# A hybrid decoder layer on one Trainium2 core: the cached index keys are gathered behind the first feed-forward block and transposed in place

## The chip, the core and the metric

The kernel runs on one core of a Trainium2 chip. The metric is the device time of one execution in microseconds. Three timed runs of the kernel before gave 1490.46, 1493.34 and 1495.22 us; their median, 1493.34 us, is the number that the change is held against. The profile is of a further execution.

The engines are named as in the profile: PE is TensorE (PEld its weight loads), DVE is VectorE, ACT is ScalarE, POOL is GpSimd and SP is SyncE. SP computes nothing here, it issues DMAs. ACT and POOL issue DMAs too. All of them run on the core's 16 DMA engines.

## The reference

One layer is computed for 512 prompt tokens and for 64 sample tokens (8 sequences with 8 new tokens each, behind a paged cache of 4096 past tokens per sequence).

```
x = x + 0.5 * SwiGLU(RMSNorm(x))                     # first feed-forward block
h = RMSNorm(x); q, k, v, qi, ki, wi, ... = h @ w_in
ki_all = concat([cache_idx_k[page_table], ki])       # sample: 4096 past index keys of 32 numbers
dots   = einsum('thd,sd->ths', qi, ki_all)           # 8 index heads
scores = einsum('th,ths->ts', wi, relu(dots))
idx    = top_k(scores)                               # 256 keys per sample token
att    = softmax(q . k[idx]) v[idx]                  # gathered from cache_k, cache_v
x = x + (gate_c * conv(h) + gate_a * att @ w_aout) @ w_o
x = x + 0.5 * SwiGLU(RMSNorm(x))                     # second feed-forward block
```

The change is about `cache_idx_k[page_table]`. It is 256 pages (8 sequences with 32 pages) of 128 keys with 32 float32 numbers, 16 KB a page, 4.19 MB together. Both feed-forward blocks are 1024 to 2816 and back, in float32.

## The kernel before, in words

The program is written out by hand for each engine: the order of the code is the order on the engine, and semaphores tie the engines together. The first 168 us, the only part that the change touches, go like this.

**The sample's feed-forward block and projections.** SP streams weights in units of 512 KB through ten slots (six of the tile `ring`, two of `w_raw`, two of `spare`), in the order in which they are used. The helper `stream` (L414) issues a unit when the semaphore `ring_used` says that the unit before in its slot was used. 82 units pass: 44 of the first matrix, 22 of the second, and 16 of `w_in`, in groups of four that here are called g0 (index columns, 296 wide, so 303 KB a unit), g1 (queries), g2 (keys) and g3 (values). On PE `stream_mm` (L635) multiplies the 64 sample rows by a unit (four matmuls in the profile's count of a 512-wide unit) and raises `ring_used`. So `ring_used` stands at 66 when the feed-forward block is through, at 70 after g0, 74 after g1 and 82 after g3. Behind unit 66 come the residual sum and the norm (DVE L2146, ACT L1453, PE L844 and L773, DVE L2087) before g0 can start.

**Work between the units.** After the first eight units PE transposes the prompt's rows (`xnp` to `xT`, L817), after units 32 it sums the prompt's squares (`prompt_sums`, L623), and after each eight units it transposes the sample's activations (`turn_a`, L782).

**The index keys.** POOL gathers one page a partition with an indirect DMA. The first gather (L2793, half of the sequences, 2.1 MB into the tile `ikn`) is issued as soon as the page table is in; the second (L2802, into the same tile) when the first half has been transposed. `turn_ik` (L795) transposes `ikn` on PE in blocks of 128x128, four to a PSUM bank, in banks 6 and 7 by turns, 16 blocks a call; there are four calls, between the units of the feed-forward block. `evac_ik` (ACT L1473) copies each bank to `ikT`.

**The small trip of the weights.** The index weights `wi` come out of g0. DVE computes the index projections (L2092 to L2191) and raises `iro_ready`. POOL then writes the weights to DRAM (`wi_scratch`, L2805) and reads them back in another layout (`wv`, L2808). DVE makes the matrices `wst` from them (L2212), then the terms of the new keys (`newrel`, L2218), and raises `S_ready`.

**The index products.** `new_dots` (L866, L869) multiplies for the new keys; its results lie in banks 4 to 7 until `newrel` is done. Then `dots(n)` for n = 0 to 15 (L886) multiplies the queries by the cached keys, banks 0 to 3 by turns, ACT takes the ReLU (L1532), and `scores_w(u)` (L897) sums the heads with `wst`. `dots` 0 to 7 need the first half of the keys, 8 to 15 the second. Behind `scores_w(3)` the prompt's first feed-forward block starts (L647).

## Time and profile before

| | us |
|---|---|
| median of three runs | 1493.34 |
| the profiled execution | 1504.95 |
| its span (first to last instruction) | 1503.2 |
| PE busy in the span | 1425.7 (95%) |
| DVE busy | 1052.6 (70%) |
| POOL busy | 592.7 (39%) |
| ACT busy | 546.1 (36%) |
| last matmul of the sample's feed-forward block ends | 118.2 |
| first matmul of the prompt's feed-forward block starts | 167.55 |

All times below are us from the start of the span. Busy shares are averages over stages with different limits: in the first 118 us the DMA engines are full and PE waits in places, from 167.55 on PE is busy nearly without a gap. A time in the table of a stage therefore says more than the 95%.

### The profile page before, as it was taken

How to read it: one execution, taken by the hardware profiler on the slowest of the kernel's cores; microseconds unless marked ns; L12 is line 12 of the kernel's file. 1: busy time of each engine (PE TensorE's matmuls, PEld its weight loads, DVE VectorE, ACT ScalarE, POOL GpSimd, SP SyncE). 2: the span in 40 equal slices, each digit the busy share in tenths (PEclk: the TensorE clock that was granted, in tenths of full speed). 3: DMA queues.
4: the chain of work that ended last, by engine and by line, in shares of the span. 5: the costliest groups of instructions: out<-in, count | busy, mean ns of one | idle time of the engine just before them, and what ended most of it. 6: DMA issues, size and time to landing. Idle time of an engine off the chain costs nothing. (4 is left out here: it accounts for less than half of the span.)

```text
span 1503.2 us, 20865 instructions
## 1 busy us (share of the span) xinstructions
PE 1425.7 (95%) x8219; PEld 1121.6 (75%) x8219; DVE 1052.6 (70%) x1684; ACT 546.1 (36%) x838; POOL 592.7 (39%) x415
## 2 busy tenths in 40 slices
PE   4998999999999999999899899899998999999998
PEld 2333578877888875436666565689998999999998
DVE  1256788989836898999996997657779755774221
ACT  1332655335712331122112234543364444453111
POOL 2000465454379855543345776122304454320000
PEclk8998999999999999999999999999999999999999
DMA  9997254232257988878458766432422323312222
GB/s 342 370 380 245 87 95 106 92 95 74 71 183 245 286 254 284 284 213 271 126 168 278 256 212 217 144 119 85 126 71 71 107 78 97 113 43 78 79 91 84
DMA packets 156930, 248.75 MB, mean 165 GB/s; under 512 B 11965, under 2 KB 104909, under 8 KB 156571
## 3 DMA queue, kind: packets, MB, share of 16 engines
q1 hardware_dynamic: 131742, 164.22, 34.1%
q0 software_dynamic: 23104, 76.16, 16.1%
q10 hardware_dynamic: 1989, 7.07, 1.2%
q8 instruction: 63, 1.03, 0.3%
q14 instruction: 32, 0.26, 0.1%
HBM read 237.58 MB, written 10.20 MB: 165 GB/s over the span
## 5 line engine op out<-in xcount | busy, mean ns | idle before, releaser
L2782 POOL TENSOR_TENSOR w_lo<-w_raw,w_hi 128x1024 fp32r<-128x1024 f32 x65 | 171.5, 2638 | 221.4 <-ACT w_hi L1330 221.1
L696 PE MATMUL ps<-bh,wqr 128*128 128x288 f32 x936 | 205.3, 295 | 4.2 <-DVE wqr L1940 2.0
L2849 POOL DMA_INDIRECT kv<-cache_v,idxT x128 | 138.6, 1083 | 96.6 <-PE ps L1108 45.7
L1330 ACT ACTIVATE w_hi<-w_raw 128x1024 fp32r<-128x1024 f32 (+1 forms) x88 | 91.3, 1037 | 227.3 <-PE ps L647 148.1
L2837 POOL DMA_INDIRECT kv<-cache_k,idxT x128 | 138.6, 1083 | 86.7 <-DVE kprod L2475 54.6
L696 PEld LDWEIGHTS ps<-bh,wqr 128*128 128x128 f32 x936 | 155.5, 188 | 5.0 <-DVE wqr L1940 3.9
L647 PE MATMUL ps<-h_hi,w_hi 128*128 128x512 f32 x352 | 139.3, 396 | 2.1 <-POOL w_lo L2782 2.1
L647 PE MATMUL ps<-h_hi,w_lo 128*128 128x512 f32 x352 | 137.4, 390 | 0.0
L647 PE MATMUL ps<-h_lo,w_hi 128*128 128x512 f32 x352 | 137.2, 390 | 0.0
L712 PE MATMUL ps<-a_hi,wqr 128*128 128x288 f32 x704 | 122.3, 295 | 0.0
L696 PE MATMUL ps<-bl,wqr 128*128 128x288 f32 x384 | 113.2, 295 | 0.0
L1093 PE MATMUL ps<-h,wn 128*128 128x288 f32 x448 | 111.1, 407 | 0.3 <-ACT sgb L1682 0.3
L1058 PE MATMUL ps<-wn,xg 128*128 128x512 f32 (+1 forms) x256 | 103.1, 563 | 4.0 <-ACT rp L1663 2.1
L1093 PEld LDWEIGHTS ps<-h,wn 128*128 128x128 f32 x448 | 84.2, 190 | 26.6 <-issue 1.9
L712 PEld LDWEIGHTS ps<-a_hi,wqr 128*128 128x128 f32 x704 | 103.1, 188 | 0.0
L1953 DVE TENSOR_TENSOR wqr<-wq,wqr 128x1024 fp32r<-128x1024 f32 (+1 forms) x24 | 27.2, 1135 | 95.1 <-ACT wqr L1368 95.1
L2914 POOL TENSOR_TENSOR wq<-wq 128x1024 f32<-128x1024 f32 x10 | 24.9, 2490 | 172.5 <-PE ps L696 76.7
L2475 DVE TENSOR_TENSOR kprod<-kv,qb 128x1024 f32<-128x1024 f32 x64 | 84.4, 1319 | 9.9 <-issue 3.3
L1058 PEld LDWEIGHTS ps<-wn,xg 128*128 128x128 f32 x256 | 49.6, 196 | 55.2 <-issue 49.0
L1215 PE MATMUL ps<-h,wn 128*128 128x288 f32 x320 | 83.9, 413 | 2.4 <-issue 2.4
L647 PEld LDWEIGHTS ps<-h_hi,w_hi 128*128 128x128 f32 x352 | 66.4, 189 | 18.1 <-issue 3.3
L2478 DVE TENSOR_REDUCE G<-kprod 128x16 f32<-128x1024 f32 x64 | 78.2, 1222 | 2.2
(513 smaller groups left out, 3190.6 us busy)
## 6 DMA issues: line engine op xcount, KB each, us to landing
w_raw<-w_ffn_in SPq DMA_DIRECT2D x56, 512.0 KB, 11.8
wq<-w_ffn_in SPq DMA_DIRECT2D x40, 512.0 KB, 3.6
wn<-w_in SPq DMA_DIRECT2D x36, 512.0 KB
qb<-q_scratch SPq DMA_DIRECT2D x64, 256.0 KB
ring<-w_ffn_in SPq DMA_DIRECT2D x28, 512.0 KB
w_raw<-w_ffn_out SPq DMA_DIRECT2D x24, 512.0 KB, 9.8
wq<-w_ffn_out SPq DMA_DIRECT2D x20, 512.0 KB
ring<-w_ffn_out SPq DMA_DIRECT2D x14, 512.0 KB
```

The source lines that it names most:

```text
L647: mm = pe.matmul(ps[:, 2 * half + m, :], w[:, k, m * P:(m + 1) * P], x[:, kc0 + k, c0:c0 + SEQ], start=(first and k == 0 and fst), stop=(l ...
L696: mm = pe.matmul(ps[:, bank + m, 0:HALF], w[:, k, m * P:(m + 1) * P], b[:, j, k, :], start=(j in (0, 1, 5) and k == 0 and fst), stop=(k == ...
L712: mm = pe.matmul(ps[:, 4 * half + 2 * m + hf_, 0:HALF], w[:, k, m * P:(m + 1) * P], x[:, kc0 + k, hf_ * HALF:(hf_ + 1) * HALF], start=(kc0 ...
L1058: mm = pe.matmul(ps[:, s % 8, 0:n], xg[:, kk, P * b:P * b + P], wt[:, k, :], start=(kk == 0), stop=(kk == KD - 1))
L1093: mm = pe.matmul(ps[:, 4 * half + 2 * m + hf_, 0:HALF], wt[:, k, m * P:(m + 1) * P], h32[:, 4 * (n % 2) + k, hf_ * HALF:(hf_ + 1) * HALF], ...
L1215: mm = pe.matmul(ps[:, hf_, 0:HALF], wt[:, k % 4, m * P:(m + 1) * P], h32[:, k, hf_ * HALF:(hf_ + 1) * HALF], start=(k == 0), stop=(k == K ...
L1330: act.activation(w_hi[:, slot, 0:n], w_raw[:, slot, 0:n], ACT.Copy).then_inc(S_("hi_ready"), 1)
L2475: dve.tensor_tensor(kprod[:, :, :], kv[:, n % KV, :, :], qb[:, j, :].unsqueeze(1).to_broadcast([P, 2, DA]), ALU.mult)\
L2478: dve.tensor_reduce(G[:, :, n], kprod[:, :, :].rearrange("p c (h d) -> p (c h) d", h=H), AX.X, ALU.add).then_inc(S_("logits_ready"), 1)
L2782: pool.tensor_tensor(w_lo[:, slot, 0:n], w_raw[:, slot, 0:n], w_hi[:, slot, 0:n].bitcast(F32), ALU.subtract)\
L2837: pool.indirect_dma_start(kv[:, n % KV, c, :], None, rows[0], bass.IndirectOffsetOnAxis(ap=idxT[:, c, n:n + 1], axis=0))\
L2849: pool.indirect_dma_start(kv[:, V_SLOT[j % 3] + a // 2, a % 2, :], None, rows[1], bass.IndirectOffsetOnAxis(ap=idxT[:, j % 2, t:t + 1], ax ...
```

## The change

The tile `ikn` goes. The gathers write straight to `ikT`, each half to its own part, and the transposes read a block of `ikT` and are copied back over the same block. The first gather is issued when `ring_used` is at 66, the second at 74 and when the first has landed. The transposes of the first half stand on PE between g0 and g1 (two calls of 16), those of the second half between the index products: 16 behind `dots(3)`, 16 behind `dots(5)`. The wait for `S_ready`, which stood behind `dots(7)`, moves with them behind `dots(3)`, since the transposes write banks 6 and 7. The transposes of the norm move to banks 4 and 5.

```diff
-        (ikn,), _ = place(m1, [("ikn", (P, PAGE * ID), F32)])
...
-                        mm = pe.transpose(ps[:, 6 + n_tr[0] % 2, j * P:(j + 1) * P], ikn[:, kg * P:(kg + 1) * P], ident[:, :])
+                        mm = pe.transpose(ps[:, 6 + n_tr[0] % 2, j * P:(j + 1) * P], ikT[:, gseq, kg, :], ident[:, :])
...
-                if t in (1, 2):
-                    turn_ik(0, 4 * t - 4)
-                if t in (4, 5):
-                    turn_ik(1, 4 * t - 16)
...
-            pe.wait_ge(S_("ikT_evac"), 16)
...
+                if g == 0:
+                    turn_ik(0, 0)
+                    turn_ik(0, 4)
...
+            pe.wait_ge(S_("ikT_evac"), 8)
             for n in range(16):
                 dots(n)
+                if n == 3:
+                    pe.wait_ge(S_("S_ready"), 1)
+                    turn_ik(1, 0)
+                if n == 5:
+                    turn_ik(1, 4)
                 if n == 7:
-                    pe.wait_ge(S_("S_ready"), 1)
+                    pe.wait_ge(S_("ikT_evac"), 16)
                     pe.wait_ge(S_("qbd_ready"), 2)
...
             act.activation(h32[:, :, 0:NS], hTs[:, :, :], ACT.Copy).then_inc(S_("hhi_ready"), 1)
+            evac_ik(0, 0)
+            evac_ik(0, 4)
...
+                if n == 3:
+                    evac_ik(1, 0)
+                if n == 5:
+                    evac_ik(1, 4)
...
-            pool.indirect_dma_start(ikn[:, :], None, ik_rows, bass.IndirectOffsetOnAxis(ap=ptile[:, 0:1], axis=0)).then_inc(S_("ik_in"), 16)
...
-            pool.wait_ge(S_("ikT_evac"), 8)
-            pool.indirect_dma_start(ikn[:, :], None, ik_rows, bass.IndirectOffsetOnAxis(ap=ptile[:, 1:2], axis=0)).then_inc(S_("ik_in"), 16)
+            for g, used_up in enumerate((66, 74)):
+                pool.wait_ge(S_("ring_used"), used_up)
+                if g:
+                    pool.wait_ge(S_("ik_in"), 16)
+                pool.indirect_dma_start(ikT[:, g, :, :].rearrange("p a b -> p (a b)"), None, ik_rows, bass.IndirectOffsetOnAxis(ap=ptile[:, g:g + 1], axis=0))\
+                    .then_inc(S_("ik_in"), 16)
 
             pool.wait_ge(S_("iro_ready"), 1)
             pool.dma_start(wi_dram, wisc[0:NS, 0, :]).then_inc(S_("wv_in"), 16)
```

In the order of the program the changed places look like this. Each row is one instruction or a run of equal ones, in the order of its engine; `[waits ...]` lists the semaphores it waits for. On PE, from the third unit of g0 (units 64x296, `hTs` is the sample's normed rows) to the start of g1, there stands before:

```order
L635 MATMUL ps<-spare,hTs 64x296 [waits ring8]
L635 MATMUL ps<-spare,hTs 64x296
L635 MATMUL ps<-spare,hTs 64x296 [waits ring9]
L635 MATMUL ps<-spare,hTs 64x296
L635 MATMUL ps<-ring,hTs 64x512 [waits ring0]
L635 MATMUL ps<-ring,hTs 64x512
L635 MATMUL ps<-ring,hTs 64x512 [waits ring1]
```

In the changed kernel the same place reads:

```order
L634 MATMUL ps<-spare,hTs 64x296 [waits ring9]
L634 MATMUL ps<-spare,hTs 64x296
L794 MATMUL ps<-ident,ikT 128x128 [waits ik_in]
L794 MATMUL ps<-ident,ikT 128x128 x7
L794 MATMUL ps<-ident,ikT 128x128 [waits ikT_evac]
L794 MATMUL ps<-ident,ikT 128x128 x3
L794 MATMUL ps<-ident,ikT 128x128 [waits ikT_evac]
L794 MATMUL ps<-ident,ikT 128x128 x3
...
L794 MATMUL ps<-ident,ikT 128x128 [waits ikT_evac]
L794 MATMUL ps<-ident,ikT 128x128 x3
L634 MATMUL ps<-ring,hTs 64x512 [waits ring0]
```

32 transposes of the first half now stand between g0 and g1, and the first one waits for the first gather (`ik_in`).

On PE among the index products (`qbd` holds the queries, `iTp` the queries for the new keys), from the end of `new_dots` to `dots(4)`, there stands before:

```order
L869 MATMUL ps<-iT,iTp 128x64 x8
L886 MATMUL ps<-ikT,qbd 128x512 x2
L886 MATMUL ps<-ikT,qbd 128x512 [waits choice_step]
...
L886 MATMUL ps<-ikT,qbd 128x512 [waits scored]
L886 MATMUL ps<-ikT,qbd 128x512
L886 MATMUL ps<-ikT,qbd 128x512 [waits scored]
L886 MATMUL ps<-ikT,qbd 128x512
L886 MATMUL ps<-ikT,qbd 128x512 [waits scored]
```

and now:

```order
L865 MATMUL ps<-iT,iTp 128x64 x8
L882 MATMUL ps<-ikT,qbd 128x512 [waits ikT_evac]
L882 MATMUL ps<-ikT,qbd 128x512
L882 MATMUL ps<-ikT,qbd 128x512 [waits choice_step]
...
L882 MATMUL ps<-ikT,qbd 128x512 [waits scored]
L882 MATMUL ps<-ikT,qbd 128x512
L794 MATMUL ps<-ident,ikT 128x128 [waits ikT_evac,ik_in,S_ready]
L794 MATMUL ps<-ident,ikT 128x128 x3
L794 MATMUL ps<-ident,ikT 128x128 [waits ikT_evac]
L794 MATMUL ps<-ident,ikT 128x128 x3
...
L882 MATMUL ps<-ikT,qbd 128x512 [waits scored]
L882 MATMUL ps<-ikT,qbd 128x512
```

The first transpose of the second half stands between `dots(3)` and `dots(4)` and waits for `S_ready` and for the second gather. Before, the products ran on here, and `S_ready` was awaited four products later.

On POOL, from the last small constant to the read of `wv`, there stood before:

```order
L2800 DMA gkb<-g_k 128x64
L2802 DMA ikn<-cache_idx_k,ptile 128x4096 [waits ikT_evac]
L2805 DMA wi_scratch<-wisc 64x8 [waits iro_ready]
L2808 DMA wv<-wi_scratch 64x8x1 [waits wv_in]
L2808 DMA wv<-wi_scratch 64x8x1
```

and now:

```order
L2803 DMA gkb<-g_k 128x64
L2808 DMA ikT<-cache_idx_k,ptile 128x4096 [waits ring_used]
L2808 DMA ikT<-cache_idx_k,ptile 128x4096 [waits ik_in,ring_used]
L2812 DMA wi_scratch<-wisc 64x8 [waits iro_ready]
L2815 DMA wv<-wi_scratch 64x8x1 [waits wv_in]
L2815 DMA wv<-wi_scratch 64x8x1
```

Between `gkb` and `wi_scratch` there are now two gathers, the second of which waits for g1; `wi_scratch` is behind it on the same queue.

## Rows read from the trace of the kernel before

**Rows 1.** The page, the span in 40 equal slices (tenths busy).

```profile
PE   4998999999999999999899899899998999999998
DMA  9997254232257988878458766432422323312222
```

**Rows 2.** Windows: length, busy us by engine (PE to POOL), PEclk, DMA, GB/s.

```profile
52.00:56.00 4.00, 4.00 (x18) 1.22 (x16) 0.76 (x2) 0.00 (x0) 0.00 (x0) 0.87 0.66 193
56.00:118.00 62.00, 57.19 (x278) 21.90 (x274) 27.01 (x39) 17.16 (x31) 1.01 (x1) 1.00 1.05 385
118.00:126.00 8.00, 2.47 (x20) 1.91 (x20) 4.92 (x9) 1.92 (x5) 0.00 (x0) 0.70 0.99 365
137.00:144.00 7.00, 7.00 (x50) 2.77 (x46) 4.51 (x8) 0.00 (x0) 1.41 (x2) 1.00 0.17 32
```

**Rows 3.** PE in time, the first 118 us (start, duration, line, tiles, wait).

```profile
48.34 1.14 PE L795 MATMUL ps<-ident,ikn 128*128 128x128 f32 x8 [2.26 <-ACT ikT L1473]
...
82.74 1.09 PE L795 MATMUL ps<-ident,ikn 128*128 128x128 f32 x8
84.09 1.14 PE L795 MATMUL ps<-ident,ikn 128*128 128x128 f32 x8 [0.25 <-ACT ikT L1473]
...
117.11 1.08 PE L635 MATMUL ps<-ring,aTs 128*64 128x512 f32 x4 [0.18 <-DMA ring<-w_ffn_out]
```

**Rows 4.** PE in time, from the norm to the prompt's first matmul.

```profile
125.93 2.24 PE L635 MATMUL ps<-w_raw,hTs 128*64 128x296 f32 x8 [0.78 <-DVE hTs L2087]
129.93 4.39 PE L635 MATMUL ps<-ring,hTs 128*64 128x512 f32 x16
134.25 0.40 PE L854 MATMUL ps<-ident,iros 64*128 64x64 f32 x3
135.08 1.94 PE L635 MATMUL ps<-ring,hTs 128*64 128x512 f32 x8
142.09 0.39 PE L866 MATMUL ps<-wisc,permm 64*128 64x8 f32 x2
143.01 1.99 PE L886 MATMUL ps<-ikT,qbd 64*128 64x512 f32 x8
...
147.52 2.04 PE L886 MATMUL ps<-ikT,qbd 64*128 64x512 f32 x8 [0.21 <-ACT relu_b L1532]
...
167.55 0.50 PE L647 MATMUL ps<-h_hi,w_hi 128*128 128x512 f32 x1
```

**Rows 5.** Windows of 46 to 130, columns as in rows 2.

```profile
46.00:48.00 2.00, 0.08 (x1) 0.00 (x0) 1.90 (x4) 0.82 (x2) 0.00 (x0) 1.00 1.06 390
50.00:52.00 2.00, 2.00 (x6) 0.69 (x8) 0.00 (x0) 0.41 (x2) 0.00 (x0) 0.50 1.00 371
122.00:130.00 8.00, 5.66 (x31) 3.23 (x31) 3.50 (x5) 1.81 (x5) 0.00 (x0) 0.50 0.71 244
```

**Rows 6.** DMA issues of the first 125 us (KB each, median us to landing).

```profile
ikn<-cache_idx_k,ptile POOLq DMA_INDIRECT x2, 11.8
permm<-c_perm POOLq DMA_DIRECT2D x1, 32.0 KB, 11.6
gkb<-g_k POOLq DMA_DIRECT2D x1, 32.0 KB, 13.3
...
wv<-wi_scratch POOLq DMA_DIRECT2D x2, 2.0 KB, 2.5
wi_scratch<-wisc POOLq DMA_DIRECT2D x1, 2.0 KB, 5.5
```

**Rows 7.** DVE in time, from the value rows to the new keys' sums.

```profile
143.91 1.66 DVE L2212 TENSOR_SCALAR wst<-spread,wv 128x128 f32<-128x128 f32 x8 [0.22 <-DVE vns L2093]
...
146.81 1.03 DVE L2223 TENSOR_REDUCE newsum<-newrel 128x64 f32<-128x512 f32 x1
```

**Rows 8.** POOL in time, the trip of the weights.

```profile
133.85 0.56 POOL L2805 DMA_DIRECT2D wi_scratch<-wisc  x1 [71.00 <-DVE iros L2187]
139.61 1.41 POOL L2808 DMA_DIRECT2D wv<-wi_scratch  x2 [5.20 <-DMA wi_scratch<-wisc]
```

More of the change, by code:

```diff
@@ L830, in _ @@
                     pe.wait_ge(S_("ones_ready"), 1)
-                    pe.wait_ge(S_("ikT_evac"), 8)
                     prompt_sums(0, 6, sqp)
@@ L841, in _ @@
             pe.wait_ge(S_("x1_ready"), 1)
-            pe.wait_ge(S_("ikT_evac"), 16)
             for k in range(KD):
-                mm = pe.transpose(ps[:, 6, k * NS:(k + 1) * NS], xs[:, k * P:(k + 1) * P], ident[0:NS, 0:NS])
+                mm = pe.transpose(ps[:, 5, k * NS:(k + 1) * NS], xs[:, k * P:(k + 1) * P], ident[0:NS, 0:NS])
             mm.then_inc(S_("hsT_done"), 1)
-            turn_h(1, 7)
+            turn_h(1, 4)
             pe.wait_ge(S_("hTs_ready"), 2)
@@ L1496, in _ @@
             silu_s(1)
-            evac_ik(0, 0)
             evac_a(0)
             silu_s(2)
-            evac_ik(0, 4)
             evac_a(1)
@@ L1504, in _ @@
             silu_s(4)
-            evac_ik(1, 0)
             evac_a(3)
             silu_s(5)
-            evac_ik(1, 4)
             evac_a(4)
@@ L1515, in _ @@
             act.wait_ge(S_("hsT_done"), 2)
-            act.activation(xT[:, :, 0:NS], ps[:, 6, :].rearrange("p (k n) -> p k n", k=KD), ACT.Copy).then_inc(S_("iTp_ready"), 1)
+            act.activation(xT[:, :, 0:NS], ps[:, 5, :].rearrange("p (k n) -> p k n", k=KD), ACT.Copy).then_inc(S_("iTp_ready"), 1)
             act.wait_ge(S_("hTs_ready"), 2)
             act.activation(h32[:, :, 0:NS], hTs[:, :, :], ACT.Copy).then_inc(S_("hhi_ready"), 1)
+            evac_ik(0, 0)
+            evac_ik(0, 4)
             act.wait_ge(S_("iT_done"), 1)
@@ L2151, in _ @@
             dve.wait_ge(S_("gm_in"), 16)
-            sample_norm(1, gmc, 7)
+            sample_norm(1, gmc, 4)
             link(dve.memset(qbd[:, :, :, :], 0.0))
```

## The prediction

> **What bounds the kernel now.** I read the page's slices first, then windows, then each engine in time. In the slices PE is at nine tenths or more nearly everywhere from the fifth slice on, while the DMA engines are full only in the first three [rows 1]. The windows say what that means. From 56 to 118 us the DMA engines are full (share 1.05) at 385 GB/s, and PE has 57.19 of 62 us [rows 2]; the last units are each waited for on a DMA [rows 3]. So up to 118.19 us (117.11 + 1.08) the bytes set the time. I call this moment E; the last matmul of the sample's feed-forward block ends there. From E to 125.93 the norm runs (DVE, ACT and PE in turns), and from there PE works through g0 to g3 and the index products to 167.55 with small gaps [rows 4]. This stretch, 49.36 us long, is a chain of PE, ACT and the small trip of the index weights. The DMA engines have holes in it: 32 GB/s from 137 to 144 us [rows 2]. Behind 167.55 PE hardly waits, and everything there (the search for the keys on DVE, the gathers of keys and values) hangs on the scores or on PE's own progress. I take it that what the start of the prompt's block moves, the end moves by the same amount.
>
> So there are two sums: how much earlier E comes, and how much longer than 49.36 us the stretch behind it becomes.
>
> **The first 118 us.** The two gathers leave. They are 2 x 128 x 16 KB = 4.19 MB, which at 385 GB/s [rows 2] is 10.9 us. With them leave 64 transposes on PE and 16 copies on ACT. These cost nothing where PE waits for DMA anyway, but once they cost something: at 46 to 48 us PE sat 2.26 us behind ACT [rows 3], its clock then stood at half level (1.2 GHz, 0.50 in 50 to 52 us) [rows 5], slots came free late, and the DMA engines moved 193 GB/s from 52 to 56 us [rows 2], a loss of 4 x (385 - 193) = 0.77 MB, 2.0 us. That stop goes too. Nothing else is late in its place: the sums of the squares stop PE for 7 us, but up to ten units are under way, ten times 0.52 MB / 385 GB/s = 13.6 us. Gain: 12.9 us, which I call at least 10.9 less a microsecond, should a new stop appear, and at most 14.
>
> **From E to the end of g1.** The norm and g0 stay: g0 ends at E + 11.7 (129.93). The first gather is issued at E. A gather beside a busy SP queue took 11.8 us to land [rows 6], and SP's queue is busy here too (365 GB/s from 118 to 126 [rows 2]), so it lands at E + 11.9. PE waits 0.2 us; bounds 0 and, with 13.3 us as for the last DMA behind a gather [rows 6], 1.6 us. The weights of g1 share the engines with it: what was still to come at E is 8 x 365 GB/s = 2.9 MB [rows 2], with the gather's 2.1 MB 5.0 MB, 13 us at 385 GB/s, so they are in before g1 needs them. The six units of g2 and g3 that are still to load, 3.1 MB, take until E + 21, and PE comes to them from E + 22 on. Then 32 transposes. 16 of them took 2.49 us (82.74 to 85.23) with ACT copying behind [rows 3], so 32 take 5.0. But after the pause of the norm the clock is at half level (0.50 from 122 to 130 us) [rows 5], and g0 pays 4.0 us for what takes half of it at full level. What g1 paid for warming up, 4.32 us (129.93 to 134.25) for what takes 3.5 (half of the 7.0 from 135.08 to 142.09) [rows 4], the transposes pay now: 0.9 more. On DVE the index projections (before under g1) now run under these transposes, and on ACT the copies are done 3 us before the next thing it is wanted for. The transposes end at E + 17.8 and g1, now 3.5 us, at E + 21.3.
>
> **To dots(3).** As before: 0.83 us of transposes (134.25 to 135.08), 7.01 for g2 and g3, 0.92 for new_dots, 4.51 for four products (143.01 to 147.52) [rows 4]: PE is behind dots(3) at E + 34.6.
>
> **The wait that the change adds.** Behind dots(3) PE now waits for S_ready, which needs newrel, which needs wst, which needs wv, which needs the trip of the weights through DRAM. Before, POOL issued the trip at 133.85, E + 15.7, and read back at 139.61 [rows 8]; wst started at 143.91, set by the value rows on DVE and not by wv (the trip was in by 139.61 + 0.7 + 2.5 = 142.8). Now POOL stands first at its wait for g1 (E + 21.3), then issues the second gather (1 us), then wi_scratch, on the same queue. DMAs issued on POOL's queue behind the first gather landed 11.6 us (the third behind it) to 13.3 us after their issue [rows 6], where small ones with nothing large ahead took 2.5 to 5.5: they came in behind the gather. So the trip waits for the second gather.
>
> How long a gather takes with the DMA engines nearly free no row shows. Below it is 2.1 MB / 385 GB/s = 5.4 us and 1.5 us of start and end (less than the 2.5 us of wv), 6.9; above it is 11.8, the one beside a full SP queue. I take 8.7, with the bytes alone and 3.3 us around them. It lands at E + 30.0, wi_scratch 1.0 later, wv 3.2 behind that (0.7 + 2.5) at E + 34.2, and wst to newrel take 2.9 (143.91 to 146.81) [rows 7]: S_ready at E + 37.2. PE stands from 34.6 to 37.2, 2.6 us. Queued behind the waiting transpose is the rest of the products, and with them scores, keys and the prompt's block.
>
> The page DMA: Bandwidth & Descriptors of the Trainium skill (section Anatomy of one DMA) gives a DMA of POOL's path 2.0 us and its bytes at 436 GB/s, which as an estimate is 6.8 us for this gather; the trace has only the 11.8 us with company, so it neither bears the rule out nor contradicts it. By it the wait would be 0.7 us, and the sum 1.9 us smaller and without the clock's share below, 1491.4 in all; that is rival 1.
>
> **From the wait to 167.55.** The 16 transposes take 2.4 us, dots(4) and dots(5) follow, then 16 more, paced by ACT, which has the ReLU and the copies in one queue: 2.6. Together 5.0 on top of the 20.03 us that the rest took (147.52 to 167.55) [rows 4]. A stop of 2.26 us was followed by half clock from about 50 to 53 us [rows 3, 5]; a stop of 2.6 us does the same here, over the transposes and two products: 1.3 us for the transposes, 1 for the products, 2.3 in all. Bounds 0 (no drop) and 4.
>
> **The sum.** The stretch is now 37.2 + 5.0 + 20.0 + 2.3 = 64.5 us against 49.36, so 15.2 longer; E is 12.9 earlier. Net +2.3 us. In the profiled execution, that is 1504.95 + 2.3 = 1507.3. It stands 11.6 us above the median of the runs; I carry the difference over: 1493.3 + 2.3 = 1495.6. A difference under 0.3%, 4.5 us, a measurement of this kernel can't tell from none.
>
> **The rivals.**
> 1. *The added wait ends early* (the gather takes 6.9 us alone, the lower bound, or wi_scratch gets past it). For it: the DMA engines are nearly idle then. Then S_ready comes at E + 35.4 at the latest, PE stops for 0.8 us or not at all, its clock stays, and without any stop 34.6 + 25.0 = 59.6, +10.2, less 12.9: -2.7 us, 1490.6. With a gain of 14 in the first part 1489.5.
> 2. *Slower: the second gather sets the path fully.* If it takes 11.8 us as beside SP's queue, S_ready comes at E + 40.3, PE stands for 5.7 us, and the clock's share is 4: 69.3, +20.0, less 12.9: +7.1, 1500.4. It decides from a landing of about 10 us on. For it: the only two gathers seen took that; against it: SP's queue has only two units of 0.5 MB left then.
> 3. *The opening gives less* (10 us, because some other stop in the stream takes over from the bytes, so that the change doesn't do there what it says). For it: the engines were not full at 52 to 56 us. Then +5.2, 1498.5.
>
> **How the numbers follow.** Forecast 0.42, rival 1 0.27, rival 2 0.17, rival 3 0.14. The forecast's own range is 1493 to 1498. The range for 8 in 10 reaches from 1489 (rival 1 with the larger gain) to 1501 (rival 2). Faster by more than 4.5 us needs rival 1 and more: 0.14. Slower by more than that: rival 2, half of rival 3, and a little of the forecast: 0.27. Within: 0.59.
>
> **What would show it.** In the changed profile: E at 105.3 and no stop near 46 us; DMA share near 1.05 up to E; the first transpose of keys within 1 us behind g0; the second gather's landing 8.7 us after its issue; wi_scratch landing behind it; wst starting on DVE behind wv and not behind the value rows; a wait of 2 to 3 us on PE ahead of the first transpose behind dots(3), put down to DVE newrel; half clock right behind it; the prompt's first matmul at 169.9. The forecast is wrong if E stays above 108, if the wait at dots(3) is missing or over 5 us, or if the part behind 168 us changes its length by more than 1 us.

## The result and the profile after

The changed kernel took 1496.98 us (median of 19 runs, 1491.98 to 1500.53) beside 1494.07 us for the kernel before on the same chip (19 runs, 1488.97 to 1498.05). The ratio is 1.0022, 95% interval 1.0013 to 1.0031: 1.9 to 4.6 us slower, which is little but more than nothing by this interval. The profiled execution of the changed kernel took 1496.92 us, its span is 1493.8.

The two rows of the page's slices look almost as in [rows 1]. No slice differs by more than a tenth but the third of PE, which fell from 9 to 7:

```profile
PE   5978999999999999999999999999998999999998
DMA  9996254322256889868448877432321322312222
```

The windows that answer to [rows 2], the third moved with the end of the sample's block:

```profile
52.00:56.00 4.00, 3.18 (x14) 0.59 (x12) 1.37 (x2) 0.63 (x1) 0.00 (x0) 1.00 1.05 388
56.00:104.00 48.00, 43.02 (x188) 13.61 (x186) 22.02 (x31) 9.32 (x16) 0.00 (x0) 1.00 1.05 377
106.00:114.00 8.00, 2.41 (x20) 1.83 (x22) 4.70 (x9) 2.45 (x5) 0.93 (x1) 0.76 1.08 420
137.00:144.00 7.00, 3.13 (x16) 1.46 (x16) 3.81 (x14) 3.52 (x6) 0.00 (x0) 1.00 0.25 78
144.00:146.00 2.00, 1.95 (x10) 1.63 (x12) 1.93 (x4) 1.16 (x3) 0.00 (x0) 0.56 0.00 0
```

The hole at 52 to 56 us is gone. From 137 to 144 us PE, which had all of the 7 us before, has 3.13. From 144 to 146 us the granted clock is 0.56. PE in time says why; these rows answer to [rows 3] and [rows 4]:

```profile
104.54 1.08 PE L634 MATMUL ps<-ring,aTs 128*64 128x512 f32 x4 [0.18 <-DMA ring<-w_ffn_out]
...
113.41 2.24 PE L634 MATMUL ps<-w_raw,hTs 128*64 128x296 f32 x8 [0.78 <-DVE hTs L2091]
...
117.35 1.09 PE L794 MATMUL ps<-ident,ikT 128*128 128x128 f32 x8
118.69 1.15 PE L794 MATMUL ps<-ident,ikT 128*128 128x128 f32 x8 [0.25 <-ACT ikT L1475]
...
122.51 3.65 PE L634 MATMUL ps<-ring,hTs 128*64 128x512 f32 x16
126.10 0.40 PE L850 MATMUL ps<-ident,iros 64*128 64x64 f32 x3
...
137.11 2.04 PE L882 MATMUL ps<-ikT,qbd 64*128 64x512 f32 x8 [0.27 <-ACT relu_a L1532]
142.70 1.09 PE L794 MATMUL ps<-ident,ikT 128*128 128x128 f32 x8 [3.55 <-DVEq L2226]
...
145.81 2.88 PE L882 MATMUL ps<-ikT,qbd 64*128 64x512 f32 x8
...
169.16 0.50 PE L646 MATMUL ps<-h_hi,w_hi 128*128 128x512 f32 x1
```

E is 104.54 + 1.08 = 105.62. The first transpose follows g0 without a wait, and the one real stop is the 3.55 us behind `dots(3)`. DVE and POOL over the same stretch answer to [rows 7] and [rows 8]:

```profile
139.84 1.65 DVE L2216 TENSOR_SCALAR wst<-spread,wv 128x128 f32<-128x128 f32 x8 [4.30 <-DMA wv<-wi_scratch]
...
142.74 1.06 DVE L2227 TENSOR_REDUCE newsum<-newrel 128x64 f32<-128x512 f32 x1
```

```profile
105.91 1.02 POOL L2808 DMA_INDIRECT ikT<-cache_idx_k,ptile  x1 [91.21 <-PE ps L634]
126.45 0.98 POOL L2808 DMA_INDIRECT ikT<-cache_idx_k,ptile  x1 [19.52 <-PE ps L634]
127.44 0.58 POOL L2812 DMA_DIRECT2D wi_scratch<-wisc  x1
135.26 1.43 POOL L2815 DMA_DIRECT2D wv<-wi_scratch  x2 [7.24 <-DMA wi_scratch<-wisc]
```

Read from the bottom up: `wv` waits 7.24 us for `wi_scratch`, which was issued right behind the second gather; `wst` waits 4.30 us for `wv`; PE waits 3.55 us for DVE. The issues' landing times, which answer to [rows 6]:

```profile
permm<-c_perm POOLq DMA_DIRECT2D x1, 32.0 KB, 5.3
gkb<-g_k POOLq DMA_DIRECT2D x1, 32.0 KB, 6.8
ikT<-cache_idx_k,ptile POOLq DMA_INDIRECT x2, 9.9
wv<-wi_scratch POOLq DMA_DIRECT2D x2, 2.0 KB, 4.1
wi_scratch<-wisc POOLq DMA_DIRECT2D x1, 2.0 KB, 7.5
```

The 9.9 is the mean of 11.4 (first gather, beside SP's stream) and 8.4 (second). `wi_scratch` took 7.5 where it took 5.5 before, and the small constants, which now have no gather ahead of them, 5.3 and 6.8 where they took 11.6 and 13.3.

### The profile page after: what moved, and what is told of

Same layout as the page of the kernel before. It is cut to its first block and busy times, and to the rows that moved or that the text cites. A ratio compares the mean times of both kernels' runs of the same rounds, so it can differ in the third digit from the quotient of the medians.

```text
span 1493.8 us, 20865 instructions
## 1 busy us (share of the span) xinstructions
PE 1424.8 (95%) x8219; PEld 1119.5 (75%) x8219; DVE 1051.3 (70%) x1684; ACT 546.0 (37%) x838; POOL 592.1 (40%) x415
```

## The experiments

"Start" is the first matmul of the prompt's feed-forward block, "stretch" is E to start. But for the two first profiles, each kernel was timed 12 times (both gathers early: 6) beside the kernel before on the same chip, in three groups of four on one chip each. Times are us from the start of the span. The runs with the second gather out, with the second half out and with the second half not transposed leave work out and compute wrong scores for half of the sequences; they serve the times only.

| kernel | ratio to before, 95% | E | stretch | start |
|---|---|---|---|---|
| before, first profile | | 118.19 | 49.36 | 167.55 |
| before, again | 0.9999 [0.9982, 1.0016] | 115.93 | 49.47 | 165.40 |
| changed, first profile | 1.0022 [1.0013, 1.0031] | 105.62 | 63.54 | 169.16 |
| changed, again | 1.0031 [1.0016, 1.0045] | 105.74 | 63.97 | 169.71 |
| trip ahead of the second gather | 0.9995 [0.9982, 1.0007] | 104.94 | 59.55 | 164.49 |
| trip on SP's queue | 1.0001 [0.9988, 1.0014] | 106.72 | 59.85 | 166.57 |
| second half not transposed | 1.0000 [0.9986, 1.0014] | 104.90 | 57.04 | 161.94 |
| both gathers early | 1.0058 [1.0038, 1.0077] | 115.05 | 59.32 | 174.37 |
| before, first calls later | 0.9990 [0.9977, 1.0002] | 115.07 | 48.88 | 163.95 |
| ... and last call in the norm's gap | 0.9995 [0.9982, 1.0008] | 115.31 | 49.19 | 164.50 |
| ... and idle products in the gap | 0.9982 [0.9971, 0.9994] | 115.19 | 48.46 | 163.65 |
| before, second gather out | 0.9981 [0.9968, 0.9995] | 114.26 | 49.21 | 163.47 |
| before, second half out | 0.9991 [0.9977, 1.0004] | 114.26 | 49.26 | 163.52 |
| one half each | 1.0020 [1.0007, 1.0033] | 113.73 | 55.52 | 169.25 |

**Both kernels again.** The changed kernel, unedited:

> The changed kernel once more, beside the kernel before on the same chip, as the base for the three others. My theory: 12.6 us less in the opening and 14.2 us more between the end of the sample's feed-forward block and the prompt's block, so about 2 to 3 us slower than before (ratio 1.0015 to 1.002). Rival (the two profiles differ by 1.6 us at the start of the prompt's block and the timed runs by 2.9, so something behind that point is slower too): ratio 1.0022 or more and a later part that is longer.

And the kernel before, unedited:

> The kernel before, unchanged, with a profile of its own beside the others. The first profile of it is 1503.2 us long, and the part behind the start of the prompt's block is 1335.6 us there, but 1324 to 1327 us in the profiles of the changed kernel and its variants, while the timed runs say that before is the faster. My theory: that first profiled execution was a slow one behind 168 us, and the part is as long in both kernels; here it is 1324 to 1327 us, the prompt's block starts at 166.5 to 167.6, and the timed ratio is 1.000. Rival: the part behind 168 us is really longer in the kernel before, again 1333 us or more, and the changed kernel gets something back there.

The changed kernel repeated its profile: E 105.74, stop 3.56 us, half clock behind it. The kernel before did not: E came 2.3 us earlier than in its first profile, and behind the start it took 1325.4 us (1490.8 - 165.40) where the first profile has 1335.6 (1503.2 - 167.55). The hole at 52 to 56 us was smaller, after the same stop of 2.26 us:

```profile
52.00:56.00 4.00, 4.00 (x20) 1.26 (x18) 1.37 (x2) 0.33 (x1) 0.00 (x0) 1.00 0.92 308
```

Over the 12 us in which the hole lies, 48 to 60, the repeat moved 356 GB/s and the first profile 317. Against 385 that is 0.35 MB and 0.82 MB, or 0.9 and 2.1 us:

```profile
48.00:60.00 12.00, 11.75 (x60) 5.64 (x59) 3.88 (x6) 3.79 (x7) 0.00 (x0) 0.88 0.99 356
```

So the first profile, on which the sum was made, shows a larger hole than the repeat does, by 1.2 us of the 2.3 us between the two E. Against the repeat the changed kernel starts the prompt's block 3.8 and 4.3 us later, and the timed medians differ by 2.9 and 3.2. Five profiles have the changed kernel's opening (its own two, the two of the trip, and the second half not transposed), and their E lies between 104.90 and 106.72. A difference of a microsecond in E can't be read from one pair of profiles alone. Most of this spread is again a hole, just behind the sums of the squares. In the order second half not transposed (E 104.90), changed (105.62) and trip on SP's queue (106.72):

```profile
64.00:76.00 12.00, 12.00 (x68) 4.95 (x69) 4.97 (x8) 1.01 (x2) 0.00 (x0) 1.00 1.07 366
64.00:76.00 12.00, 12.00 (x64) 4.88 (x64) 4.37 (x7) 1.01 (x2) 0.00 (x0) 1.00 1.04 347
64.00:76.00 12.00, 12.00 (x62) 4.76 (x63) 4.16 (x7) 1.01 (x2) 0.00 (x0) 1.00 1.03 322
```

Against 385 GB/s these lack 0.6, 1.2 and 2.0 us. The kernel before has no such hole there: its repeat moved 401 GB/s in the same 12 us, with the second gather under way.

**The trip of the weights ahead of the second gather.** On POOL only the order is changed:

```diff
+            pool.wait_ge(S_("ring_used"), 66)
+            gather_ik(0)
             pool.wait_ge(S_("iro_ready"), 1)
             pool.dma_start(wi_dram, wisc[0:NS, 0, :]).then_inc(S_("wv_in"), 16)
...
+            pool.wait_ge(S_("ring_used"), 74)
+            pool.wait_ge(S_("ik_in"), 16)
+            gather_ik(1)
```

> The changed kernel, with the trip of the index weights through DRAM issued on POOL's queue before the second gather. My theory: the trip is late because POOL stands first at its wait for g1 and then because the small DMAs land behind the gather; with the order turned, wst is set by the value rows again, PE doesn't stop at dots(3) (3.55 us in the changed kernel), its clock stays at full level there (about 1.2 us), and the second gather, issued 1.4 us later, still lands before dots(3) ends. So 4.7 us less than the changed kernel, ratio to before about 0.999. Rival: the wait at dots(3) is for the gather of the second half itself (it takes 8.4 us), then the stop stays at 2 us or more.

```profile
120.64 0.56 POOL L2813 DMA_DIRECT2D wi_scratch<-wisc  x1 [14.39 <-DVE iros L2191]
125.67 1.42 POOL L2816 DMA_DIRECT2D wv<-wi_scratch  x2 [4.46 <-DMA wi_scratch<-wisc]
127.38 1.02 POOL L2806 DMA_INDIRECT ikT<-cache_idx_k,ptile  x1 [0.30 <-issue]
```

On DVE, and on PE the first transposes behind `dots(3)`:

```profile
135.94 1.66 DVE L2216 TENSOR_SCALAR wst<-spread,wv 128x128 f32<-128x128 f32 x8 [0.22 <-DVE vns L2097]
```

```profile
139.27 1.09 PE L794 MATMUL ps<-ident,ikT 128*128 128x128 f32 x8
```

`wst` again stands behind the value rows, as in [rows 7], PE does not stop, the clock stays, and the gather, issued 0.9 us later, is still in before its transposes. The stretch is 4.0 and 4.4 us shorter than in the two profiles of the changed kernel, and the timed ratio is back at 1. This shows that the place on POOL's queue costs the changed kernel about all that it loses. Two things change together, and this run doesn't part them: the write is issued 6.8 us sooner (120.64 instead of 127.44), since POOL no longer waits for g1 first, and it lands 4.7 us after its issue instead of 7.5.

**The trip on SP's queue.** SP, which streams the weights, issues it behind the last of them instead of POOL:

```diff
+            sp.wait_ge(S_("iro_ready"), 1)
+            sp.dma_start(wi_dram, wisc[0:NS, 0, :]).then_inc(S_("wv_in"), 16)
+            sp.wait_ge(S_("wv_in"), 16)
...
-            pool.wait_ge(S_("iro_ready"), 1)
-            pool.dma_start(wi_dram, wisc[0:NS, 0, :]).then_inc(S_("wv_in"), 16)
```

> The changed kernel, with the trip of the index weights issued by SP, which is through with its weights by then, and both gathers issued on POOL exactly as in the changed kernel. My theory: the trip lands 3 to 5 us after its issue although the gathers fill the engines, since it is no longer behind them in one queue; no stop at dots(3); 4.7 us less than the changed kernel. Rival (the trip is late since the engines are full, not since it is queued): the trip's write takes 7 us here too, S_ready comes about 2 us earlier only because POOL's wait is gone, and the stop stays at 1 us or more.

SP came to it only when slots were free for its last loads. The write went out 1.55 us ahead of the second gather (127.45), and the read back ran beside it:

```profile
125.90 0.48 SPq L483 DMA_DIRECT2D wi_scratch<-wisc  x1
130.20 1.65 SPq L486 DMA_DIRECT2D wv<-wi_scratch  x2
```

The two reads of `wv` landed 5.6 and 7.9 us after their issue, `wst` began at 138.83 behind a wait of 2.30 us for them, PE stopped for 1.55 us, and the clock did not fall. This is not the same trip on another queue, however: SP's version breaks it into 1040 packets more. Up to 150 us the profile counts 27111 packets here, 2944 of them under 512 B, against 26071 and 1904 in the changed kernel, for the same bytes. From 134.5 to 138 us, with all but 0.08 MB of the gather through, over a thousand packets under 512 B still passed. So the late read doesn't show what a gather's company costs a small transfer, nor does this run show that `wi_scratch` would land sooner beside a gather on another queue.

**The second half not transposed.** In the changed kernel both calls of the second half and their copies are out; the waits for `S_ready` and for the second gather stay. Products 8 to 15 multiply untransposed keys.

```diff
                 if n == 3:
                     pe.wait_ge(S_("S_ready"), 1)
-                    turn_ik(1, 0)
-                if n == 5:
-                    turn_ik(1, 4)
+                    pe.wait_ge(S_("ik_in"), 32)
```

> The changed kernel without the transposes of the second half and their copies on ACT; the waits for S_ready and for the second gather stay behind dots(3) (the products 8 to 15 multiply keys that are not transposed). My theory: the transposes between the products are worth 5.0 us on the path and the stop is a cost of its own, so the stop at dots(3) stays at 3.5 us, the clock falls all the same, and the prompt's block starts 4 to 5 us earlier than in the changed kernel, at about 164.7; ratio to before about 0.9995. Rival: the transposes are half hidden behind ACT's ReLU, then it starts only 2.5 us earlier.

```profile
136.42 2.04 PE L882 MATMUL ps<-ikT,qbd 64*128 64x512 f32 x8 [0.27 <-ACT relu_a L1529]
141.90 1.99 PE L882 MATMUL ps<-ikT,qbd 64*128 64x512 f32 x8 [3.44 <-DVEq L2219]
```

From 141.90 to the start it took 20.04 us, against 26.46 (142.70 to 169.16) in the changed kernel: 6.4 us, where 4 to 5 were expected. Without a stop, in the kernel with the trip ahead of the gather, 25.22 us pass from the end of `dots(3)` to the start, so the transposes are 5.2 us of it, and the clock the other 1.2. (In the repeat of the changed kernel the clock's share is 0.7 by the same sum: 169.71 - 143.82 = 25.89.) The clock stayed up here, after a stop of 3.44 us:

```profile
138.00:144.00 6.00, 2.45 (x12) 0.69 (x8) 4.57 (x15) 2.46 (x3) 0.00 (x0) 1.00 0.00 0
```

The timed ratio of 1.0000 is not as low as the start, 3.5 us earlier than before's, would make it; that is the one place where start and time part by more than 1.2 us, and it stays open.

**The first calls of transposes one round later,** in the kernel before (and the copies with them):

```diff
-                if t in (1, 2):
-                    turn_ik(0, 4 * t - 4)
+                if t in (2, 3):
+                    turn_ik(0, 4 * t - 8)
```

> The kernel before, with the first two calls of the transposes moved one round of eight units later, and their copies on ACT with them. My theory: the stop of PE at 46 us and the hole of the DMA engines at 52 to 56 us (0.77 MB, 2.0 us) are the second term of the gain in the opening, apart from the bytes. Without the stop the end of the sample's feed-forward block comes 2.0 us earlier and the whole is 2 us faster than before (ratio 0.9987). Rival (only the bytes of the gathers count): no change.

```profile
48.00:60.00 12.00, 11.75 (x64) 4.94 (x62) 4.90 (x8) 3.08 (x6) 0.00 (x0) 1.00 1.05 387
```

The stop and the slow clock behind it are gone, the hole too, and E is 0.9 us earlier than in the repeat of before. That is as much as the repeat's own hole is worth, so 0.9 us is taken as what the stop of [rows 3] costs there; the sum had 2.0, from the larger hole of the first profile.

**The second gather left out,** in the kernel before. The second half is transposed from the rows of the first, so half of the sequences are scored with other keys.

```diff
-            pool.indirect_dma_start(ikn[:, :], None, ik_rows, bass.IndirectOffsetOnAxis(ap=ptile[:, 1:2], axis=0)).then_inc(S_("ik_in"), 16)
```

> The kernel before without its second gather; the second half of the keys is transposed from the first half's rows, so all work of PE and ACT stays and only 2.1 MB of DMA leave (the scores of half of the sequences are of other keys). My theory: the bytes set the end of the sample's block, 2.1 MB at 385 GB/s are 5.4 us, so the block ends at 112.8, the prompt's block starts at 162.1, and the ratio to before is 0.9964. Rival: PE with its transposes and stops has a share in the bound, then 3 us or less.

2.1 MB less, 5.4 us at 385 GB/s, moved E by only 1.7 us. A hole opened elsewhere:

```profile
72.00:84.00 12.00, 11.75 (x54) 4.75 (x53) 4.03 (x6) 1.83 (x4) 0.00 (x0) 1.00 0.89 280
```

PE is busy throughout; my reading is that it gives slots back late, so that SP can't issue. In these 12 us the DMA engines could have moved 4.62 MB (385 GB/s) and moved 280 x 12 = 3.36 MB. The missing 1.26 MB are 3.3 us, where the repeat of before (368 GB/s) lacks 0.5. The hole at 52 to 60 was larger as well (314 GB/s against 349), by 0.7 us. Together 3.5 us, nearly the 3.7 that E lacks.

**The second half out of the opening altogether,** in the kernel before: neither gathered nor transposed; products 8 to 15 use the first half's keys.

```diff
-                if t in (4, 5):
-                    turn_ik(1, 4 * t - 16)
...
-            pool.indirect_dma_start(ikn[:, :], None, ik_rows, bass.IndirectOffsetOnAxis(ap=ptile[:, 1:2], axis=0)).then_inc(S_("ik_in"), 16)
```

> The kernel before without the second gather and without the 32 transposes of the second half (products 8 to 15 multiply the first half's keys again, so half of the sequences are scored with other keys). With only the gather taken out E came 1.7 us earlier where its bytes are 5.4 us, and the DMA engines had a hole at 72 to 84 us. Theory (the hole was PE's doing: the transposes and the sums of the prompt's squares kept PE from giving slots back): with the transposes gone as well the bytes bind again, E comes 5.4 us earlier than in the repeated run of the kernel before, at about 110.5, no hole over 1 us worth at 72 to 84, prompt's first matmul at 159.9, ratio 0.9963. Rival (the sums of the squares alone bind there): E at 112.5 to 113.5, the hole stays, ratio 0.998.

My theory fell: E is 114.26 as in the run above, and most of the hole is there.

```profile
72.00:84.00 12.00, 12.00 (x58) 4.65 (x58) 3.69 (x6) 1.01 (x2) 0.00 (x0) 1.00 0.94 308
```

That the two E agree to the hundredth is chance. The hole is 2.4 us here and 3.3 above, where the first 16 of the second half's transposes (81.85 to 84.27) fall into its end; in return the hole at 52 to 60 us, in which the two kernels do the same work, was larger here (293 GB/s against 314), by 0.4 us. By these holes the second half's 32 transposes cost half a microsecond to one, and what makes most of the hole is ahead of them: the sums of the squares, and perhaps the first half's transposes.

**Both gathers early, transposes as changed.** From the changed kernel:

```diff
             ik_rows = inp["cache_idx_k"].rearrange("o n p d -> (o n) (p d)")
+            gather_ik(0)
...
+            pool.wait_ge(S_("ring_used"), 32)
+            pool.wait_ge(S_("ik_in"), 16)
+            gather_ik(1)
```

> The changed kernel with one thing undone: both gathers are issued in the opening (the first when the page table is in, the second when 32 units of the stream are used), while the 64 transposes stay where the change puts them. The trip of the index weights then has no gather ahead of it on POOL's queue. Theory (the trade is bytes in the opening against transposes in the stretch, and the second gather's place costs a stop of 3.6 us and a slow clock of 1.2 us on top): E, the end of the sample's feed-forward block, goes back by both gathers' bytes, to 115.5 to 116.5 us; no stop behind dots(3); E to the prompt's first matmul takes what the kernel with the trip ahead of the second gather took, 59.5 us; the prompt's first matmul at 175 to 176; ratio to the kernel before 1.006 to 1.007. Rival (without the transposes in the opening PE gives slots back soon enough that part of the gathers' bytes passes unseen): E at 112 to 113, prompt's first matmul at 172, ratio 1.004.

E goes back by 9.4 us (105.62 to 115.05; 9.3 from the repeat), between theory and rival and nearer to the theory. Behind `dots(3)` PE went on at once:

```profile
147.18 2.04 PE L882 MATMUL ps<-ikT,qbd 64*128 64x512 f32 x8 [0.27 <-ACT relu_a L1532]
149.16 1.09 PE L794 MATMUL ps<-ident,ikT 128*128 128x128 f32 x8
```

The bytes of two gathers are 10.9 us. Of the other 1.5, 1.1 pass in time that the stream could not use: the changed kernel's DMA engines moved 370 GB/s from 64 to 90 us, those of this kernel 386, which is 0.42 MB more:

```profile
64.00:90.00 26.00, 23.36 (x102) 8.28 (x104) 9.76 (x15) 4.09 (x7) 0.84 (x1) 1.00 1.05 386
```

**One half each.** The first half is gathered and transposed in the opening (its calls one round later), the second half is gathered when `ring_used` is at 66, ahead of the trip, and transposed between the products.

```diff
+            gather_ik(0)
...
+                if t in (2, 3):
+                    turn_ik(0, 4 * t - 8)
...
+            pool.wait_ge(S_("ring_used"), 66)
+            gather_ik(1)
             pool.wait_ge(S_("iro_ready"), 1)
             pool.dma_start(wi_dram, wisc[0:NS, 0, :]).then_inc(S_("wv_in"), 16)
```

> One half as before, one half as changed: the first half is gathered and transposed in the opening (its two calls one round later than before), the second half is gathered at the end of the sample's feed-forward block, ahead of the trip of the index weights on POOL's queue but with the whole of g0 to g3 before its transposes, which stand between the products. Theory (each half costs about 5.4 us of bytes in the opening or about 5.2 us of transposes in the stretch, so that where it stands is nearly the same): E at 110.4, stretch 54.7, prompt's first matmul at 165.1, no stop behind dots(3) over 1 us, ratio 0.9993 to 1.0. Rival (the trip queued behind the gather is late here too, wi_scratch landing 7 us or more after its issue, and stops PE behind dots(3) by 2 us or more): prompt's first matmul at 167 to 168, ratio 1.001. Other rival (with half the transposes gone from the opening PE also spares the stops there): E at 109, ratio 0.998.

Both rivals and the theory missed: no stop behind `dots(3)`, but E only at 113.73, 3.3 us later than the bytes say, and the kernel is slower than before. (In the stretch PE also waits 1.0 us for the last weights of g3.) The stream from 64 to 90 us, in the changed kernel (first) and in this one:

```profile
64.00:90.00 26.00, 24.62 (x124) 8.57 (x122) 15.90 (x22) 6.88 (x11) 0.00 (x0) 1.00 1.05 370
```

```profile
64.00:90.00 26.00, 25.08 (x128) 10.91 (x125) 10.24 (x15) 6.17 (x11) 0.00 (x0) 1.00 0.95 324
```

And what PE does there:

```profile
63.68 1.09 PE L794 MATMUL ps<-ident,ikT 128*128 128x128 f32 x8
...
66.90 7.10 PE L622 MATMUL ps<-sqp,ones 128*128 128x512 f32 x16 [0.34 <-issue]
```

Transposes and sums keep PE from the stream for 10.3 us in a row (63.68 to 73.94). The sums alone, in the changed kernel, left 370 GB/s. With the same transposes and sums and the second gather issued at 66.73, right at the sums (the kernel before with the first calls later), it was 386. The gather needs no slot, so its bytes can pass just then. In the repeat of before it is issued 7 us ahead of the sums and still under way in them:

```profile
60.87 1.01 POOL L2802 DMA_INDIRECT ikn<-cache_idx_k,ptile  x1 [44.98 <-ACT ikT L1473]
```

So the gather fills the hole that transposes and sums make. With neither in the opening E is at 105.6; with one gather and 32 transposes at 113.7, 8.1 us more; with both halves (first calls later) at 115.1, only 1.3 more, where the second gather's bytes are 5.4. The reading that each half costs the same wherever it stands is wrong: 8.1 and 1.3 us are further apart than the 1.8 by which E varies.

**The last call in the norm's gap.** From the kernel with the first calls later:

```diff
-                if t in (4, 5):
-                    turn_ik(1, 4 * t - 16)
+                if t == 5:
+                    turn_ik(1, 0)
...
+            turn_ik(1, 4)
             pe.wait_ge(S_("x1_ready"), 1)
```

> The kernel of e3 (the kernel before with the first two calls one round later), with the last call of 16 transposes moved behind the last unit of the sample's feed-forward block, where PE waits for the residual sum and the norm. My theory: PE's clock falls to half level since PE has next to nothing to do from 118 to 126 us, and g0 pays 2 us and g1 0.8 us for it; the transposes are free there and shorten the pause, so the clock stays up or is back sooner, and the prompt's block starts 1.5 to 2.8 us earlier than in e3, ratio 0.9975. Rival: what is left of the pause (3 us and more with 16 small transposes in it) still brings the clock down, no gain over e3.

E did not move (115.31 beside 115.07), and 2.5 us of work at the head of the gap did not hold the clock (0.57 over 120 to 128 us, 0.62 without it). The rival held.

**Idle products in the gap,** on the same base: 18 ahead of the first transposes of the norm, 10 behind them and 4 behind the second ones (the profile counts two for each).

```diff
+            idle_products(18)
             pe.wait_ge(S_("x1_ready"), 1)
...
+            idle_products(10)
             turn_h(1, 7)
+            idle_products(4)
```

> The kernel before with the two first calls of transposes one round later, and 32 idle 128x128 products of PE (results unused, written to a bank that is free) in the pauses of the norm behind the sample's feed-forward block; their number fills most of the pauses of about 6 us. Theory (the half clock under g0 and g1, 0.50 from 122 to 130 us before, comes from PE's pause in the norm): the granted clock stays at 2.4 GHz, g0 and g1 together take 2.0 to 2.8 us less, E unchanged at 115, stretch 46.9, prompt's first matmul at 161.5, ratio 0.9973. Rival 1 (the clock falls in spite of idle products, since they leave pauses between them): same as without them, ratio 0.999. Rival 2 (g0 is held by ACT and DVE or by its weights, not by the clock): clock up, but g0 and g1 start no earlier and end within 1 us of before, ratio 0.9985.

```profile
122.00:130.00 8.00, 7.96 (x56) 4.21 (x54) 5.75 (x14) 0.63 (x1) 0.00 (x0) 1.00 0.70 244
```

```profile
119.34 0.71 PE L850 MATMUL ps<-ident,xs 64*128 64x64 f32 x8
119.98 2.50 PE L844 MATMUL ps<-ones,ident 128*128 128x128 f32 x20
122.41 0.71 PE L773 MATMUL ps<-ident,hns 64*128 64x64 f32 x8
...
124.13 1.22 PE L635 MATMUL ps<-w_raw,hTs 128*64 128x296 f32 x8
```

The granted clock is 1.00 throughout, where the same kernel without the products had 0.50 from 120 to 126 us, and g0 takes 2.05 us (124.13 to 126.18) where it took 3.65 there (122.82 to 126.47). That is 1.6 us (g1 takes 3.60 in both), less than the 2.0 to 2.8 expected of the two, and the products stood in the way: the norm's first transposes began 4.2 us behind E instead of 3.2, and g0 8.9 instead of 7.7 us behind it. So 1.2 us of the 1.6 went there, and the stretch is only 0.4 us shorter than without them. This kernel has the lowest ratio of those that compute everything, 0.9982 to before; its interval overlaps that of the same kernel without the products (0.9990), so the timed runs don't show the 0.4 us. Fewer products might keep more of it; that wasn't tried.

## Why the prediction was right, and where a size was off

The forecast was 1495.6 us, slightly slower than before and within 0.3% of it; the kernel took 1496.98 beside 1494.07. The chain from E to the prompt's block was the forecast one. The gain of the opening was not.

- *E 12.9 us earlier.* 12.57 against the first profile, but 10.2 and 10.3 against the repeat. This is the mis-sized term, by 2.6 us against the repeat. Bytes: 10.9 predicted, 9.4 measured (both gathers early). The stop near 46 us: 2.0 predicted, 0.9 measured (first calls later). 9.4 + 0.9 = 10.3; each is a difference of two profiles, while E of one and the same opening varied by 1.8. Two steps failed. One priced the whole low rate at 52 to 56 us from one profile [rows 2]. The other put the sums of the squares at nothing ("nothing else is late in its place", since ten units under way would last 13.6 us): the five profiles of the changed opening lack 0.5 to 2.0 us of bytes just behind the sums, a hole that the second gather filled before. So the bytes were not the bound everywhere.
- *First gather in at E + 11.9, PE waits 0.2.* It landed at 117.3, E + 11.7, and no matmul of PE waited for it.
- *Transposes 5.0 + 0.9, g1 out at E + 21.3.* 5.16 us for the 32 in the first profile (117.35 to 122.51) and 5.93 in the repeat (117.68 to 123.61), where the clock came back later. g1 ended at E + 20.5 and + 21.5, `dots(3)` at E + 33.5 and + 34.5 (predicted 34.6).
- *Second gather 8.7 us.* 8.4. The rule of the Trainium skill (DMA: Bandwidth & Descriptors, section Anatomy of one DMA), 6.8 by the estimate made from it, was 1.6 us too low: the measurement decides.
- *`wi_scratch` 1.0 behind it, `wv` 3.2, then 2.9.* 7.5 us from issue, so it came in almost with the gather; from `wv`'s issue to `wst` 4.6 us (135.26 to 139.84) instead of 3.2; 2.9 from `wst` to `newsum`. These errors nearly cancel: S_ready at E + 37.1, predicted 37.2 (E + 38.1 in the repeat, with g1 a microsecond later).
- *Stop 2.6 us, clock 2.3.* 3.55 and 1.2 (3.56 and 0.7 in the repeat). Both ends of the stop hang on the end of g1, so an earlier or later g1 doesn't change it. From there S_ready took 16.6 us in both profiles where the sum had 15.9, and PE was behind `dots(3)` after 13.05 where it had 13.3. The clock stayed down over fewer instructions. Together 4.75 and 4.2 against 4.9. With the trip ahead of the gather the stop is 0 and the stretch 59.6 (the 59.6 that the prediction gives for the case without a stop).
- *Stretch 64.5.* 63.5 and 64.0.
- *Net +2.3.* +1.6 against the first profile and +3.8 to +4.3 against the repeat; +2.9 and +3.2 by the timed runs. That the number came out so close is partly luck: the opening gave 2.6 us less than the sum had, and the stretch, 14.1 and 14.5 us longer instead of 15.2, took back 0.7 to 1.1 of it.
- *What the start moves, the end moves.* Good as a rule, not exact: behind the start the 13 profiles other than the first took 1323.0 to 1328.2 us, the longer ones where the start was early (1328.2 from 161.94, 1323.1 from 174.37). The prediction called itself wrong if this part changed by more than 1 us. From the first profile of before (1335.6) to the changed kernel (1324.6) it changed by 11; the repeat of before (1325.4) shows that this was the first profile's own, and against it the change is 0.8 and 1.2 us. The timed differences follow the start within 1.2 us except in the one case named. What takes up the rest wasn't sought.

Of the rivals, the added wait did not end early (rival 1: stop at most 0.8 us); the gather did not take its 11.8 (rival 2); the opening did give less, as rival 3 had it (10 us; 10.2 and 10.3 against the repeat), and in part by its mechanism, a place where something other than the bytes binds the stream. The place was the sums of the squares, which stood there before too. So the forecast was right for the stretch and rival 3 for the opening.

## What to carry to other kernels

Look whether a small transfer that the critical path waits for can be issued ahead of a large one on the same queue: here that order alone gave about 4 us back. Where a stream is full, ask not only how many bytes leave it but what held its slots meanwhile: a transfer that needs no slot can run while the consumer is busy elsewhere, so the second gather hid in part behind transposes and sums, and taking it out gave 1.3 to 1.7 us instead of 5.4. Before a hole in one profile is priced, look whether a second profile of the same kernel shows it.

## What the runs showed of the hardware that I had not expected

- A pause of PE is not always followed by half clock. After 2.26 us (kernel before) and 3.55 and 3.56 us (changed) the granted clock went to about 0.5 for some 3 us; after 3.44 us (second half not transposed) and 1.55 us (trip on SP) it stayed at 1.00. What PE did behind the pause differed: transposes in the cases where it fell, products of 512 columns or, behind 1.55 us, transposes where it did not. The length of the pause alone does not decide.
- Idle 128x128 products in the norm's gap held the clock at 1.00 through a stretch that had 0.50 without them (120 to 126 us), where 2.5 us of transposes at its head did not.
- A 2 KB write issued behind a 2.1 MB gather on the same queue landed 7.5 us after its issue in all three profiles that have this order, about with the gather. Ahead of the gather it took 4.7, and 2.3 to 5.5 in the others. Whether the queue or the gather's share of the DMA engines made it late wasn't parted.
- The two 2 KB reads that bring `wi_scratch` back in another layout took 2.5 to 4.4 us from POOL's queue and 5.6 and 7.9 us from SP's, where the trip made 1040 packets more. The gather beside them took 11.0 us instead of 8.1 to 8.4.
- The gather itself took 8.1 to 8.4 us with little else under way and 10.6 to 12.3 beside SP's full stream.
